# One hybrid S5 and attention layer on one core: the root of x, the second scan and the third S5 quarter in another order

## What is computed

```python
hn = rms_norm(h, norm_mix[l])
proj = hn @ w_in[l]
u_ssm = proj[..., :D_SSM]                 # q, k, v are the other three slices
y_ssm = s5_mixer(u_ssm, ...)              # a complex linear scan over time, 32 groups
y_att = moba_attention(q, k, v, rel_bias)
mixed = jnp.concatenate([rms_norm(y_ssm, ...), rms_norm(y_att, ...)], axis=-1)
h = h + mixed @ w_out[l]
h = h + memory_cross_attention(...)
h = h + conv_ffn(...)
```

## Time and profile before

| | |
|---|---|
| median of 3 runs | 670.17 us (669.82 to 670.47) |
| the profiled execution | 670.81 us, its span 668.8 us |
| mean granted clock of PE | 0.997 of 2.4 GHz |
| PE busy | 656.2 us (98%) |
| DVE busy | 487.2 us (73%) |
| ACT busy | 340.6 us (51%) |
| POOL busy | 172.5 us (26%) |
| from 20 to 100 us, DVE and POOL busy | 76.2 and 75.7 of 80 us |

### The profile page before, as it was taken

The page is one execution under the profiler, slowest core; times in us unless marked ns, Lnnn a source line. Parts: engine busy times, 40 slices in busy tenths (PEclk is TensorE's granted clock), DMA queues, the critical chain, the costliest instruction groups (busy, mean ns, idle before and its releaser), DMA issues.

```text
span 668.8 us, 10548 instructions
## 1 busy us (share of the span) xinstructions
PE 656.2 (98%) x3914; PEld 542.1 (81%) x3914; DVE 487.2 (73%) x801; ACT 340.6 (51%) x587; POOL 172.5 (26%) x177
## 2 busy tenths in 40 slices
PE   8899999999999999999999999999999999999997
PEld 7688778877888788887998888888888888888886
DVE  5998998578766665557697666666656687868967
ACT  6538564766745464764354333334334345554662
POOL 4998992223220102330000111011110121100000
PEclk9999999999999999999999999999999999999999
DMA  8868515666120404030357555564566446655663
GB/s 296 309 206 130 167 44 145 177 185 221 64 66 1 158 2 188 4 124 0 127 189 249 199 182 188 192 225 151 186 222 218 151 170 223 211 189 140 182 196 125
DMA packets 67737, 106.99 MB, mean 160 GB/s; under 512 B 15792, under 2 KB 40496, under 8 KB 66288
## 3 DMA queue, kind: packets, MB, share of 16 engines
q1 hardware_dynamic: 64528, 100.17, 45.9%
q10 hardware_dynamic: 3168, 6.29, 2.9%
HBM read 89.54 MB, written 15.73 MB: 157 GB/s over the span
## 4 chain that ended last, share of the span: by engine, by line
PE 80%; DVE 11%; ACT 3%; SPq 2%; DMA 2%; issue 1%; POOL 1%; ACTq 0%; DVEq 0%
PE pb L510 23%; PE pb L512 23%; PE pb L511 23%; PE pb L1962 6%; PE pb L1965 4%; DVE F L1384 3%; DVE wring L500 2%; ACT F L993 1%; DMA raw<-in_w_in 1%; SPq L664 1%; DMA F<-scr_y 1%; DVE F L1390 1%; DVE pb L1384 1%; DVE sq L1432 1%; DVE wring L1384 1%
## 5 line engine op out<-in xcount | busy, mean ns | idle before, releaser
L510 PE MATMUL pb<-xs,wring 128*128 128x512 f32 (+1 forms) x400 | 149.6, 374 | 0.7 <-POOL xs L911 0.7
L512 PE MATMUL pb<-xs,wring 128*128 128x512 f32 (+1 forms) x400 | 148.9, 372 | 0.0
L511 PE MATMUL pb<-xs,wring 128*128 128x512 f32 (+1 forms) x400 | 148.9, 372 | 0.0
L1390 DVE SCALAR_TENSOR_TENSOR F<-pb,cols,F 128x511 f32<-128x511 f32 x88 | 65.9, 748 | 71.6 <-ACT F L993 69.7
L500 DVE TENSOR_TENSOR wring<-raw,wring 128x1024 fp32r<-128x1024 f32 x70 | 93.4, 1336 | 8.0 <-ACT wring L489 7.9
L510 PE MATMUL pb<-wring,xs 128*128 128x512 f32 x240 | 98.5, 411 | 0.3 <-DVE wring L503 0.3
L993 ACT ACTIVATE F<-pb,cols 128x512 f32<-128x512 f32 x50 | 38.2, 767 | 115.3 <-PE pb L512 115.2
L512 PE MATMUL pb<-wring,xs 128*128 128x512 f32 x240 | 93.9, 391 | 0.0
L511 PE MATMUL pb<-wring,xs 128*128 128x512 f32 x240 | 93.7, 390 | 0.0
L510 PEld LDWEIGHTS pb<-xs,wring 128*128 128x128 f32 x400 | 75.3, 188 | 14.1 <-issue 1.3
L512 PEld LDWEIGHTS pb<-xs,wring 128*128 128x128 f32 x400 | 75.3, 188 | 13.2
(11 more groups left out here) (152 smaller groups left out, 1011.1 us busy)
## 6 DMA issues: line engine op xcount, KB each, us to landing
raw<-in_ffn_w_up SPq DMA_DIRECT2D x22, 1024.0 KB, 5.3
F<-in_ffn_w_down SPq DMA_DIRECT2D x11, 1024.0 KB, 4.9
scr_w<-F SPq DMA_DIRECT2D x11, 1024.0 KB, 3.9
F<-in_x SPq DMA_DIRECT2D x8, 512.0 KB, 8.6
raw<-in_w_in ACTq DMA_DIRECT2D x4, 1024.0 KB, 6.3
raw<-in_w_out SPq DMA_DIRECT2D x4, 1024.0 KB, 4.9
raw<-scr_w SPq DMA_DIRECT2D x8, 512.0 KB, 3.8
raw<-scr_w SPq DMA_DIRECT2D x15, 256.0 KB, 4.7
```

The source lines that it names most:

```text
L510: nc.tensor.matmul(ps, lh, rh, start=first, stop=False)
L511: nc.tensor.matmul(ps, lh, rl_, start=False, stop=False)
L512: return nc.tensor.matmul(ps, ll, rh, start=False, stop=last)
L1390: return V.scalar_tensor_tensor(out=o, in0=a, scalar=s1, in1=b, op0=o1, op1=o2)
```

## The change

On POOL the power of x goes ahead of one subtraction (`bc[:, 1]`), and the first table waits for `xr_ready`; later the power of mk goes behind the halving. On DVE the mean of x goes between the products and the sums of the last doubling, the two products of `turns(0)` are cut apart (the second stands behind `split_lo(4)`), and `split_lo(5)` goes ahead of the next turns; `scan(1)` goes ahead of `split_lo(11)`, and `skip_in(2)` ahead of `split_lo(19)`. On SP, for q = 2, `y_write` goes ahead of chunk 10, `y_back` ahead of `t_load(3)`, and the bias load behind both.

```diff
@@ sync
             for q in range(NQ - 1):
+                y_write(q)
                 if q == 2:
                     load_chunk(sync, 10)
-                y_write(q)
+                    y_back(q)
                 t_load(q + 1)
-                if q == 2:
-                    bias_load()
-                y_back(q)
+                if q < 2:
+                    y_back(q)
+
+            bias_load()
@@ gpsimd
             nc.gpsimd.tensor_tensor(bc[:, 0], bb[:, 0], bb[:, 1], ALU.add).then_inc(sums_ok, 1)
-            sub(bc[:, 1], bb[:, 1], bb[:, 0]).then_inc(sums_ok, 1)
             pool.wait_ge(half_ok, 1)
...
             pow_event(EVN["x"])
+            sub(bc[:, 1], bb[:, 1], bb[:, 0]).then_inc(sums_ok, 1)
             pool.wait_ge(pw_ready, 1)
+            pool.wait_ge(xr_ready, 1)
...
-            pow_event(EVN["mk"])
             pool.wait_ge(zz_ready, NQ)
             nc.gpsimd.tensor_scalar_mul(sg[:, 2, :], uT[:, 3, :], 0.5).then_inc(half_ready, 1)
+            pow_event(EVN["mk"])
             glu_input(3)
@@ vector
                 if step == 0:
-                    tt(ta, c(21).unsqueeze(2).to_broadcast(shape), steps, ALU.mult)
+                    link(tt(ta, c(21).unsqueeze(2).to_broadcast(shape), steps, ALU.mult))
+                if step == 1:
                     link(tt(tb, c(22).unsqueeze(2).to_broadcast(shape), steps, ALU.mult))
-                if step == 1:
+                if step == 2:
                     link(tt(tc, ta, tb, ALU.add))
...
                 link(tt(t[3], a[1], b[0], ALU.mult))
+                if m == 4:
+                    dve.wait_ge(sq_done, TT)
+                    mean_sq("x")
                 tt(pw[:, 0, :, m + 1:2 * m + 1], t[0], t[1], ALU.subtract)
...
-            dve.wait_ge(sq_done, TT)
-            mean_sq("x")
             dve.wait_ge(pw_ready, 1)
             turns(0)
             root("x", xr_ready)
             split_lo(dve, U_Q)
+            turns(1)
...
             for m in range(4):
                 u_evac(m)
-            turns(1)
             split_lo(dve, U_Q + 1)
+            turns(2)
             split_lo(dve, U_Q + 2)
-            turns(2)
+            turns(3)
             split_lo(dve, U_Q + 3)
-            turns(3)
+            turns(4)
...
             head_rows("q", qk, range(TT), H, HD)
+            scan(1)
             split_lo(dve, 11)
-            scan(1)
             split_lo(dve, 12)
...
             scan(3)
+            skip_in(2)
             split_lo(dve, 19)
-            skip_in(2)
             split_lo(dve, 20)
```

More of the change, by code:

```diff
@@ L1492, in turns @@
                 if step == 0:
-                    tt(ta, c(21).unsqueeze(2).to_broadcast(shape), steps, ALU.mult)
+                    link(tt(ta, c(21).unsqueeze(2).to_broadcast(shape), steps, ALU.mult))
+                if step == 1:
                     link(tt(tb, c(22).unsqueeze(2).to_broadcast(shape), steps, ALU.mult))
-                if step == 1:
+                if step == 2:
                     link(tt(tc, ta, tb, ALU.add))
                     link(V.tensor_scalar_add(tc, tc, MAGIC))
-                if step == 2:
+                if step == 3:
                     link(stt(tc, tc, MAGIC, ta, ALU.subtract, ALU.subtract))
                     link(tt(tb, tb, tc, ALU.subtract))
-                if step == 3:
+                if step == 4:
                     link(ts(tb, tb, 0.4999999, -0.4999999, ALU.min, ALU.max))
```

## The result

The changed kernel is slower: a median of 674.57 us (673.05 to 675.31, 6 runs) against 670.00 us for the kernel before beside it, a ratio of 1.0066 (95% interval 1.0055 to 1.0076). The time lies above the whole range of the prediction. The profiled execution took 674.62 us, its span 672.7 us, against 670.81 and 668.8.

The account below looks back on a forecast made before the run. TensorE, busy 98% of the span, bounds the kernel, so only its pauses can be won back. Terms +0.4 + 1.4 - 1.3 - 1.75 - 0.6 = -1.85 from 670.17 give 668.3 us, range 666.2 to 671.0.

Parts of the forecast that it names:

- the second scan: scan(1) ahead of split_lo(11) on DVE: PE's 0.9 us wait goes; with the 0.4 at kernels_in(1), -1.3 us.
- the 0.4: At kernels_in(1), PE's 0.4 us wait for a bank ACT empties goes because PE comes later; counted in the -1.3.
- Part 1: Root of x sooner: PE's 2.59 us pause goes, but later waits give +0.4 and +1.4; second scan gives -1.3.
- the wait for bank 0: At the first q projection, PE waits for u_evac(0) on DVE: a 1.6 us pause, start at 32.3 us.
- `ca(0)`: POOL's table, ready at 52.4 us, 2.4 later than before; PE waits 2.7 us for it at kernels_in(0).
- replay of turns: POOL and DVE alternate instructions, so POOL's queue from the root's end R to the table's end takes 23.5 us.
- +0.4: At kernels_in(0), PE's wait for the POOL table uses up the root's gain and leaves PE 0.4 us later.
- +1.4: Behind PE's 2.7 us pause before kernels_in(0), the clock drops to 0.50, costing 1.4 us.
- pause and its clock: The old pause for the root of x and the low clock behind it cost 2.6 + 1.4 = 4.0 us.
- Part 2: SyncE queue: y_back(2) goes out sooner, ending PE's pauses between 130 and 160 us: -1.75 and -0.6 us.
- rival 3: The second part does nothing: y_back(2) lands late behind chunk 10's 1 MB, DVE stands at skip_in(2): 670.7 us, chance 0.10.
- rival 4: Slower: t_load(3)'s small transfers land behind y_back(2)'s packets and PE stops 2.2 us: 671.9 us, chance 0.10.

Follow-up runs that it names:

- kernel two: The kernel before with only scan(1) put ahead of split_lo(11): 675.82 us, ratio 1.0099.
- kernel one: The changed kernel with one swap undone, split_lo(11) ahead of scan(1) on DVE again: 667.68 us, ratio 0.9966.
- kernel five: The kernel before with only the moves around the root of x, including POOL's wait for xr_ready: 669.83 us, ratio 1.0001.
- kernel three: The changed kernel, scan(1) still ahead, with ACT's load of chunk 7 behind the four evacuations of q transposes: 667.86 us, ratio 0.9969.
- kernel seven: Kernel three without POOL's wait for xr_ready ahead of the first table: 667.57 us, ratio 0.9969.
- kernel four: The kernel before with only the new SyncE order for q = 2, skip_in(2) ahead of split_lo(19), power of mk behind the halving: 668.05 us, ratio 0.9973.
- Kernels six and eight: Six: kernel three with kernels_in(0) two tiles later on PE, 666.06 us. Eight: six with y_out(0) ahead of split_hi(11) on ACT, 665.91 us.

## Why the prediction was wrong

**The step that failed** is the second scan: "its price is `split_lo(11)`, which PE wants only after outputs(1), 2.2 us later". I asked when PE wants the split unit, and not who else waits for the split. ACT's load of chunk 7 does, and `qt_evac(0)` stands behind it. In place of -1.3 the swap costs +6.0 (kernel two). The prediction named no rival with this mechanism; its slower one was at the Toeplitz load, where nothing went wrong. Without the swap (kernel one) the change gives 667.7, within 0.6 us of the 668.3 forecast. That it comes so close is in part luck: the forecast has its -1.3 from the swap, and kernel one saves the same two waits without the swap, because PE comes later.

**The -1.3 wasn't there to win either.** 0.92 and 0.35 of it vanish in kernels one and five with the scan where it was, because PE comes later. The clock rows behind kernel three, in the last section, leave 0.7 us for the executions in which PE isn't late. Otherwise the two savings were the same microseconds, and the prediction saw that for the 0.4 but not for the 0.9: a PE that is 1.8 us late needs no scan 2.2 us sooner.

**Part 1 was right in its steps.** The root ended at 28.58 (forecast 28.9), the wait for bank 0 came at 32.02 with 1.35 (32.3, 1.6), `ca(0)` at 51.93 (52.4) with a PE pause of 2.52 (2.7), low clock behind it. The replay of turns held as a whole: from the root's end to the end of `ca(0)` it took 23.35 us, forecast 23.5. Its list of POOL's instructions has 13 entries where it says 12, and its 2.3 us for two 512-wide sums are 2.6 by the earlier trace rows, too small to matter. Kernel seven shows the part of the new wait: 1.7 us of `ca(0)`. `kernels_in(0)` came at -0.09 for +0.4. The clock's +1.4 measured 1.63 in the profile (from -0.09 to +1.54), and 0, 0.7 and 1.5 us of the whole time in kernels five, one and three (last section). In after itself the four executions with a mean clock of 0.992 took 674.9 us in the mean, the two with 0.995 took 673.3: 1.5 us, if the difference is this low stretch. The sum of this part without the scan, 1.8 late at outputs(0), measured 1.42 to 1.54, and by outputs(1) it had been absorbed (kernel five: a ratio of 1.0001).

**The 4.0 us of "pause and its clock" was oversized.** The clock's 1.4 behind the old pause cost nothing: kernel four came to `kernels_in(0)` 0.18 later without it, and that is how much later its whole trace lies (23.20 against 23.05). This didn't change the sum, which went by `ca(0)`, but it made the pause look like a larger prize than it was.

**Part 2 was right**: -2.35 forecast, -1.8 measured alone (interval -2.5 to -1.1), and -2.43 in the profile of after (+6.44 at outputs(3), +4.01 at the GLU). That the whole gain comes from the sooner `y_back(2)`, as the prediction has it, is not shown, since kernel four moves several things at once. PE is busy 30.00 of 30 us. In after the reading back goes out at 122.90, not 116, since all of it is some 6 us late, and y(2)'s own write and chunk 10 stand ahead of it. It still ends (126.5) before the Toeplitz load (127.41), whose place behind PE's outputs is unmoved: neither rival 3 nor rival 4 came.

**The account.** +0.0 at `kernels_in(0)`, +1.5 for its clock, -0.4 at `kernels_in(1)`, then +3.7 and +2.5 for the pause at the q transposes and its clock, -0.9 at outputs(1), -2.4 in part 2: +4.0, where the two profiled executions differ by 3.8.

## What to carry to other kernels

Before moving a step past another, list everybody who waits on its semaphore, a DMA issue in another engine's queue included, and then what stands behind that waiter in its queue: here a load of weights that nobody needed for long held the one evacuation that PE needed at once. Let the trace price it: look at when the waiter ran before (78.83) against when its releaser ended (78.75), and if it is the same moment there is no cover. Two savings that follow each other on the path aren't added before asking whether the first one's remainder already covers the second, and the same holds for a low clock: its price is what is late behind it.

## What the runs showed of the hardware

**A pause of some 2 to 2.5 us lowers the clock in some executions and not in others.** Behind the root's pause of 2.59 us in the kernel before the granted clock was 0.50, behind that of 2.56 us in kernel four it was 1.00. Of 38 executions of the kernel before 15 had a mean clock of 0.997 (room for one low stretch) and 17 of 1.00; two had 0.999 and four 0.994 or 0.995. Kernel four had 0.997 in 7 of 10. Kernel three, with the pause of 2.5 at `ca(0)`, had 0.997 in 8 and 1.00 in 2, kernel one with the same pause 3 and 5. In kernel seven a pause of 1.92 was followed by 0.50, in kernel two one of 1.78 was not. Kernels six and eight, whose pauses in the S5 stage are at most 1.2 us, had 0.999 or 1.00 in all eight. All ten executions of after (pause of 3.8) and kernel two (5.0) had means of 0.992 to 0.995, and both profiled ones have the low clock at that pause. For the other eight this is argued only, since four executions of the kernel before came to 0.994 or 0.995 without such a pause in its profile.

**What a low stretch costs depends on what is late behind it.** In the kernel before, the executions with it had a mean of 669.7 us and those without of 670.1 in the first batch, 670.0 and 669.9 in the second: nothing. Behind the pause for `ca(0)` it cost nothing in kernel five (669.7 with it in 4, 670.5 without in 5 executions), 0.7 us in kernel one (668.0 in 3, 667.3 in 5) and 1.5 us in kernel three (668.0 in 8, 666.6 in 2). The order fits what stands behind: in kernel five all of PE's old waits for ACT and the scan, in kernel three neither the load nor the scan, so that a PE that keeps its clock can keep its lead. In kernel seven the two executions with a mean of 0.997 took 667.4 us and the four with 1.00 took 667.5: nothing. These are few executions, and no trace of kernels one, three or five with the clock held was taken, so this stays argued. If it holds, the sooner scan is worth up to 0.7 us where the clock holds. Why the same pause lowers the clock in one execution and not in another is open.

**A row on DVE and a row on POOL hold each other up where both read from SBUF.** Five instructions of `ca(0)` take 10.4 us in after (41.49 to 51.93), 2.1 each, beside DVE's splits and turns. One of the same size took 1.17 us at 94.51, with DVE idle, and two 512-wide products took 2.08 us together at 32.03, beside DVE's evacuations from PSUM. In kernel seven the last step of the root, four elements wide, took 0.90 us beside a POOL product, and 0.16 in after beside an idle POOL.
